# Residual rows placed in PSUM ahead of the first expert, XR as a weight slot, and other orders on VectorE and ScalarE around the groups of heads

## The reference

```python
x = x + g1 * yx                                  # residual of the first block
h2 = modulate(rms_norm(x, norm2_g), sh2, sc2)
x = x + g2 * expert_choice_moe(h2, w_router, w_gate, w_up, w_down)
x = rms_norm(x, final_g)

def expert_choice_moe(h, w_router, w_gate, w_up, w_down):
    aff = softmax(h @ w_router)                  # 256 tokens x 16 experts
    top_w, top_i = top_k(aff.T, 32)              # 32 tokens of each expert
    xg = h[top_i]
    y = (silu(xg @ w_gate) * (xg @ w_up)) @ w_down
    return zeros.at[top_i].add(y * top_w)

def hybrid_mixer(h, ...):                        # each layer of the second block
    z = h @ w_in
    o_mla = mla_attention(q_nope, q_rope, k_nope, k_rope, v_mla)
    o_dil = dilated_attention(rope(qd), rope(kd), vd)
    return concat([rmsnorm(o_mla), rmsnorm(o_dil)]) @ w_out
```

## Time and profile before

| | |
|---|---|
| median of 3 runs | 2342.73 us (2342.62 to 2346.84) |
| the profiled execution's own time | 2353.84 us, span 2352.5 us |
| mean granted clock of TensorE | 0.902 |
| PE busy | 2030.9 us, 86% |
| VectorE busy | 960.3 us, 41% |
| ScalarE busy | 650.2 us, 28% |
| DMA | 647.46 MB, mean 275 GB/s |
| chain that ended last | PE 52%, DMA 34%, VectorE 8% |

### The profile page before, as it was taken

How to read it: one execution, slowest core, us unless ns; L and a number is a source line. 1 busy time by engine, 2 the same in 40 slices (tenths; PEclk the granted TensorE clock), 3 DMA queues, 4 the chain that set the end, 5 groups by cost and what they waited for, 6 DMA issues and landing times.

```text
span 2352.5 us, 29084 instructions
## 1 busy us (share of the span) xinstructions
PE 2030.9 (86%) x12314; PEld 1353.1 (58%) x12314; DVE 960.3 (41%) x1182; ACT 650.2 (28%) x779; POOL 67.4 (3%) x144
## 2 busy tenths in 40 slices
PE   7999999666666666666778999999999999999998
PEld 4767862111111111111136998778998999778997
DVE  3744431000000000000004657866658666876656
ACT  3423210000000000000003444545445444455444
POOL 0000000000000000000001000000001000100000
PEclk9999999787777777777789999989999999999999
DMA  7355789999999999999998564325554554415552
GB/s 301 118 186 193 301 339 405 420 421 420 420 421 421 421 420 420 421 421 421 420 421 323 190 213 155 130 99 180 191 194 153 189 196 161 177 50 199 200 183 95
DMA packets 91361, 647.46 MB, mean 275 GB/s; under 512 B 10144, under 2 KB 10656, under 8 KB 14304
## 3 DMA queue, kind: packets, MB, share of 16 engines
q1 hardware_dynamic: 91232, 645.61, 70.3%
HBM read 644.52 MB, written 1.05 MB: 274 GB/s over the span
## 4 chain that ended last, share of the span: by engine, by line
PE 52%; DMA 34%; DVE 8%; SPq 2%; ACT 1%; issue 1%; POOL 0%; DVEq 0%; ACTq 0%; POOLq 0%
PE PS L429 13%; PE PS L431 13%; PE PS L430 13%; DMA ring<-in_md 6%; DMA ring<-in_mu 6%; DMA ahead<-in_mu 2%; DMA XT<-in_mu 2%; SPq L2752 2%; PE PS L913 2%; DVE low L1798 2%; PE PS L818 1%; PE PS L784 1%; DMA QT<-in_md 1%; DMA HRI<-in_md 1%; DMA XT<-in_md 1%
## 5 line engine op out<-in xcount | busy, mean ns | idle before, releaser
L1798 DVE TENSOR_TENSOR low<-ring,WH 128x2048 fp32r<-128x2048 f32 (+1 forms) x163 | 372.1, 2283 | 181.1 <-ACT WH L2185 178.5
L429 PE MATMUL PS<-XH,WH 128*128 128x256 f32 x1408 | 396.5, 282 | 3.6 <-DVE XL L1829 3.6
L430 PE MATMUL PS<-XL,WH 128*128 128x256 f32 x1408 | 395.0, 281 | 0.0
L431 PE MATMUL PS<-XH,low 128*128 128x256 f32 x1408 | 393.0, 279 | 0.0
L2185 ACT ACTIVATE WH<-ring 128x2048 fp32r<-128x2048 f32 (+1 forms) x164 | 313.3, 1911 | 27.1 <-DMA ring<-in_fg 21.6
L429 PEld LDWEIGHTS PS<-XH,WH 128*128 128x128 f32 x1408 | 264.5, 188 | 7.2 <-issue 5.4
L431 PEld LDWEIGHTS PS<-XH,low 128*128 128x128 f32 x1408 | 267.2, 190 | 0.0
L430 PEld LDWEIGHTS PS<-XL,WH 128*128 128x128 f32 x1408 | 264.3, 188 | 1.4
L1780 DVE TENSOR_TENSOR T1S<-T1S,PS 128x512 f32<-128x512 f32 x16 | 11.0, 688 | 532.1 <-PE PS L878 532.1
L2435 ACT ACTIVATE T1S<-PS 128x512 f32<-128x512 f32 x16 | 9.6, 597 | 548.6 <-PE PS L878 548.6
L429 PE MATMUL PS<-WH,FH 128*128 128x512 f32 x352 | 139.7, 397 | 0.4 <-DVE FL L1927 0.4
(11 more groups left out here) (435 smaller groups left out, 3033.4 us busy)
## 6 DMA issues: line engine op xcount, KB each, us to landing
ring<-in_fg SPq DMA_DIRECT2D x44, 1024.0 KB, 4.9
ring<-in_fu SPq DMA_DIRECT2D x44, 1024.0 KB, 4.9
ring<-in_fd SPq DMA_DIRECT2D x44, 1024.0 KB, 4.8
ring<-in_md SPq DMA_DIRECT2D x43, 1024.0 KB, 27.1
ring<-in_mu SPq DMA_DIRECT2D x39, 1024.0 KB, 27.0
ring<-in_mg SPq DMA_DIRECT2D x38, 1024.0 KB, 27.5
ring<-in_wmod SPq DMA_DIRECT2D x24, 1024.0 KB, 6.5
ahead<-in_mg SPq DMA_DIRECT2D x14, 1024.0 KB, 27.3
```

What stands on the lines that cost most here:

```text
L429: t.matmul(o, l[0], r[0], start=start, stop=False, skip_group_check=True)
L430: t.matmul(o, l[0], r[1], start=False, stop=False, skip_group_check=True)
L431: return t.matmul(o, l[1], r[0], start=False, stop=stop, skip_group_check=True)
L1798: own(v.tensor_tensor(low[:, w.slot.index, 0:size], w.flat, WH[:, w.slot.index, 0:size].bitcast(f32), ALU.subtract).then_inc(*c.wl.up()), ...
```

## The change

The residual rows are added into banks 4 to 7 ahead of the first expert, as the products that open the sums (`start=True`), while VectorE selects the tokens; all experts then add to them. For this the banks 4 to 7 must be free then: the router's logits move to banks 0 and 2, the transposed softmax to bank 1, and the gathered rows to banks 1, 2 and 3, the second half of them evicted by VectorE alone. The fillers around these steps are 3, 12 and 3 where they were 8, 28 and 3. XR is then free during the experts and becomes the twentieth slot of `rest`, behind XT; its semaphore is that of the later row loads, which count on from it.

In the second block VectorE splits the fifth tile of `wid` behind the rotation of q instead of ahead of q's eviction, and the third and fourth tile of `wo2` in the groups 8 and 10 instead of 6 and 8, behind `low_rows`. ScalarE writes the high part of the first half of the rows (`rows(0, 0, 4)`) ahead of the second half of the values instead of behind it. PE transposes the first `dilated_heads` into bank 6 and then bank 7 instead of 7 and 6, so that ScalarE gets the first pair of heads and VectorE the second.

The diff, with its context cut and twelve columns of indentation taken off:

```diff
--- before.py
+++ after.py
@@ -293,7 +293,8 @@
 (ATG[:, 0:2048], c.l_ctx, (c.xr, 4), 1),
-(flat(XT[:, :, :]), c.wide6, (c.rt, 3)))]
+(flat(XT[:, :, :]), c.wide6, (c.rt, 3)),
+(flat(XR[:, :, :]), c.l_row, (c.wo, 9)))]
@@ -352,9 +353,10 @@
 load_expert(slot)
-        rest = wide[4:10] + slots + wide[10:13] + wide[0:4]
+        rest = wide[4:10] + slots + wide[10:14] + wide[0:4]
         for n in range(384 - 8):
 load_expert(rest[n % len(rest)])
+        row_slot[0].loads = wide[13].loads
         last_load = {id(s): n for n, w in enumerate(queue) for s in narrow if s.last is w}
@@ -802,7 +804,7 @@
     for k in range(4 * h, 4 * h + 4):
-        x = t.matmul(PS[:, 4 + m, 0:16], XT[:, k, m * 128:m * 128 + 128], wrA[:, k, :],
+        x = t.matmul(PS[:, 2 * m, 0:16], XT[:, k, m * 128:m * 128 + 128], wrA[:, k, :],
                      start=k == 0, stop=k == 7, skip_group_check=True)
@@ -820,8 +822,6 @@
             if n == 1 and m == 1 and k == 3:
-                take(4)
-                take(5)
                 logits(0, 0)
@@ -833,22 +833,28 @@
 logits(1, 1)
-for b in range(3):
-    held[b] = [(c.xta, 8)]
-held[3] = [(c.xtv, 7)]
-take(7)
-turn_over(6, 8)
+held[0], held[1], held[2], held[3] = [(c.rtv, 1)], [(c.xta, 8)], [(c.rtv, 2)], [(c.xtv, 7)]
+take(1)
+turn_over(6, 3)
 P.wait_ge(c.rtv, 3)
 for m in range(2):
-    x = t.transpose(PS[0:16, 7, m * 128:m * 128 + 128], aff[:, m, :], ident)
+    x = t.transpose(PS[0:16, 1, m * 128:m * 128 + 128], aff[:, m, :], ident)
 x.then_inc(*c.rt.up())
-turn_over(6, 28)
+turn_over(6, 12)
+
+P.wait_ge(c.xna, 4)
+for m in range(2):
+    for n in range(2):
+        take(4 + 2 * m + n)
+        x = t.matmul(PS[:, 4 + 2 * m + n, :], ident[:, :], XR[:, m, n * 512:n * 512 + 512],
+                     start=True, stop=False, skip_group_check=True)
+x.then_inc(*c.wo.up())
 take(3)
...
 x.then_inc(*c.rt.up())
-turn_over(6, 3)
+turn_over(0, 3)
@@ -861,7 +867,7 @@
 for k in range(8):
-    x = gather(k, 0, 2, (6, 5, 2, 4)[k // 4 * 2 + k % 2], (k % 4) // 2 * 64)
+    x = gather(k, 0, 2, 3 if k > 3 else 2 - k % 2, k * 64 - 128 if k > 3 else k // 2 * 64)
     if k % 4 == 3:
@@ -873,7 +879,7 @@
                 P.wait_ge(c.xgv, 1 + k // 4)
-                P.wait_ge(c.xga, 1 + k // 4)
+                P.wait_ge(c.xga, 1)
             for j in range(4):
@@ -883,14 +889,14 @@
                 if k > 1:
-                    P.wait_ge(*((c.xga, 2 + k // 2) if k % 2 else (c.xgv, 2 + k // 2)))
+                    P.wait_ge(*((c.xga, 1 + k // 2) if k % 2 else (c.xgv, 2 + k // 2)))
                 else:
...
         P.wait_ge(c.xgv, 6)
-        P.wait_ge(c.xga, 6)
+        P.wait_ge(c.xga, 5)
     P.wait_ge(c.rp, ex + 1)
@@ -918,18 +924,12 @@
             turn_over(3, 6)
-    if ex == 2:
-        P.wait_ge(c.xr, 4)
-        for m in range(2):
-            for n in range(2):
-                t.matmul(PS[:, 4 + 2 * m + n, :], ident[:, :], XR[:, m, n * 512:n * 512 + 512],
-                         start=False, stop=False, skip_group_check=True)
     P.wait_ge(c.pw, ex + 1)
...
             x = t.matmul(PS[:, 4 + 2 * m + n, :], PB[:, 0, m * 128:m * 128 + 128], T1[:, n * 512:n * 512 + 512],
-                         start=ex == 0, stop=ex == 15, skip_group_check=True)
+                         start=False, stop=ex == 15, skip_group_check=True)
         if n or ex == 15:
@@ -1077,7 +1077,7 @@
             x.then_inc(*c.dq.up())
-            held[at] = [(c.dqa if b else c.dqv, 2 * l + i + 1)]
+            held[at] = [(c.dqa if b == i else c.dqv, 2 * l + i + 1)]
@@ -1150,7 +1150,7 @@
     latent_heads()
-    dilated_heads(0, (7, 6))
+    dilated_heads(0, (6, 7))
@@ -1670,7 +1670,7 @@
     lg = aff[:, m, :]
-    own(v.scalar_tensor_tensor(lg, PS[:, 4 + m, 0:16], stat[:, m:m + 1], cB, ALU.mult, ALU.add))
+    own(v.scalar_tensor_tensor(lg, PS[:, 2 * m, 0:16], stat[:, m:m + 1], cB, ALU.mult, ALU.add))
     own(v.tensor_reduce(r1[:, m:m + 1], lg.rearrange("p (h e) -> p h e", h=1), X, ALU.max,
@@ -1702,7 +1702,7 @@
 R = T2[0:16, :].rearrange("p (a b) -> p a b", a=4)
-av = PS[0:16, 7, 0:256]
+av = PS[0:16, 1, 0:256]
 eq, w_, gt, w2 = (R[:, i, :] for i in range(4))
@@ -1731,10 +1731,16 @@
 own(one_hot(1, 0, 2).then_inc(*c.oh.up()), c.oh)
-for h in range(2):
-    V.wait_ge(c.gx, h + 1)
-    own(second_affine(4 * h, XG0[:, 4 * h, :], PS[:, 6 - 4 * h, 0:64]))
-    own(second_affine(4 * h + 2, XG0[:, 4 * h + 2, :], PS[:, 6 - 4 * h, 64:128]).then_inc(*c.xgv.up()), c.xgv)
+V.wait_ge(c.gx, 1)
+own(second_affine(0, XG0[:, 0, :], PS[:, 2, 0:64]))
+own(second_affine(2, XG0[:, 2, :], PS[:, 2, 64:128]).then_inc(*c.xgv.up()), c.xgv)
+V.wait_ge(c.gx, 2)
+for k in range(4, 8):
+    i = second_affine(k, XG0[:, k, :], PS[:, 3, k * 64 - 128:k * 64 - 64])
+    if k == 7:
+        own(i.then_inc(*c.xgv.up()), c.xgv)
+    else:
+        own(i)
 for m in range(2):
@@ -1994,8 +2000,9 @@
     def dilated_heads(i, b):
-        V.wait_ge(c.dq, 4 * l + 2 * i + 1)
-        own(v.tensor_copy(DT[:, i, 0:2, :].rearrange("p a b -> p (a b)"), PS[:, b, :]).then_inc(*c.dqv.up()), c.dqv)
+        h = 0 if i else 2
+        V.wait_ge(c.dq, 4 * l + 2 * i + h // 2 + 1)
+        own(v.tensor_copy(DT[:, i, h:h + 2, :].rearrange("p a b -> p (a b)"), PS[:, b, :]).then_inc(*c.dqv.up()), c.dqv)
@@ -2034,7 +2041,6 @@
     dilated(1, 0, 6)
-    split_to(tile("wid", 6 * l) + 5)
     q_up(0, 2)
@@ -2045,6 +2051,7 @@
             own(i)
+    split_to(tile("wid", 6 * l) + 5)
     latent_heads()
@@ -2106,10 +2113,10 @@
             normed({4: 1, 8: 5, 10: 7}[g])
-        if g in (2, 4, 6, 8):
-            split_to(tile("wo2", 4 * l) + g // 2)
         if g in (6, 10):
             low_rows(g // 10, 0, 0 if g == 10 else 4)
+        if g in (2, 4, 8, 10):
+            split_to(tile("wo2", 4 * l) + {2: 1, 4: 2, 8: 3, 10: 4}[g])
         if g == 5:
@@ -2420,10 +2427,9 @@
-for h in range(2):
-    A.wait_ge(c.gx, h + 1)
-    own(second_affine(4 * h + 1, XG0[:, 4 * h + 1, :], PS[:, 5 - h, 0:64]))
-    own(second_affine(4 * h + 3, XG0[:, 4 * h + 3, :], PS[:, 5 - h, 64:128]).then_inc(*c.xga.up()), c.xga)
+A.wait_ge(c.gx, 1)
+own(second_affine(1, XG0[:, 1, :], PS[:, 1, 0:64]))
+own(second_affine(3, XG0[:, 3, :], PS[:, 1, 64:128]).then_inc(*c.xga.up()), c.xga)
 for ex in range(16):
@@ -2522,8 +2528,9 @@
     def dilated_heads(i, b):
-        A.wait_ge(c.dq, 4 * l + 2 * i + 2)
-        own(copy(DT[:, i, 2:4, :].rearrange("p a b -> p (a b)"), PS[:, b, :]).then_inc(*c.dqa.up()), c.dqa)
+        h = 2 if i else 0
+        A.wait_ge(c.dq, 4 * l + 2 * i + h // 2 + 1)
+        own(copy(DT[:, i, h:h + 2, :].rearrange("p a b -> p (a b)"), PS[:, b, :]).then_inc(*c.dqa.up()), c.dqa)
@@ -2598,14 +2605,16 @@
             exps(g + 1)
+        if g == 6:
+            rows(0, 0, 4)
         if g in (2, 6):
...
             squared(g // 9, g // 7 % 2 if g < 9 else 0)
-        if g in (6, 10, 11):
-            rows(*{6: (0, 0, 4), 10: (1, 0, 0), 11: (0, 1, 1)}[g])
+        if g in (10, 11):
+            rows(*{10: (1, 0, 0), 11: (0, 1, 1)}[g])
     squared(1, 1)
...
     def ple_rows(i):
```

## The result

| | before | after |
|---|---|---|
| median of 8 runs each, same chip | 2346.05 us (2341.25 to 2351.81) | 2336.27 us (2334.17 to 2338.53) |
| profiled execution | 2353.84 us, span 2352.5 | 2335.08 us, span 2333.8 |
| mean granted clock | 0.902 | 0.908 |

The ratio is 0.9958, interval 0.9945 to 0.9971: faster, by 0.4%. The prediction was 2334.5 us, range 2330 to 2341. Between the two profiled executions the span fell by 18.7 us, as the sum had it; between the medians the time fell by 9.8 us, where I had 8.3.

The account below looks back on a forecast made before the run. It took the weight stream to bound the experts, and PE with its waits the second block. Terms: 18.7 us off the profiled execution gives 2335.1, 8.3 off the 2342.73 median gives 2334.4; forecast 2334.5 us, range 2330 to 2341.

Parts of the forecast that it names:

- 18.7: Whole kernel: predicted gain in us against the profiled execution, 3.3 + 2 x 0.8 + 2 x 1.7 + 10.4.
- The stream: First expert: XR as twentieth slot and an earlier restart close the weight stream's gap, gaining 3.3 us.
- my head start of 1.2: Router: with fewer fillers the softmax transposes, selection and first expert come 1.2 us earlier.
- The split behind q: Second block, both layers: moving VectorE's split behind q's rotation removes PE's 0.82 us wait, gaining 0.8 us a layer.
- The bank swap: Second block, first dilated_heads: swapping banks 6 and 7 gains 0, at most 0.3 us.
- The XL order: Head group with XL: the new order removes 1.9 of PE's 2.00 us wait; less 0.2 new waits, 1.7 a layer.
- The clock: Behind the XL wait, both layers: without the wait no falls to half clock are expected, gaining 10.4 us.
- the two theories: Experiments' question: each part gives its wait's cost (the sum), or clock dominates and nearly all comes from the XL order.
- no fall behind the waits of 0.2 to 1.0 us: Rival, second block: the clock falls anyway, there or behind another PE wait of about 1 us; 2343.3 us, chance 0.13.
- PE not late to the first expert: Rival, first expert: PE comes late by what the tile bought, the stream gains nothing; 2337.8 us, chance 0.08.
- VectorE not the bound: Rival, head groups: VectorE becomes the bound and the 1.7 us a layer don't come; 2337.9 us, chance 0.08.
- no wait at the last copy: Rival, last copy of turned weights: the split delays it, PE waits up to 2 us, clock falls; 2356 us, chance 0.05.

Follow-up runs that it names:

- heads_only: The kernel before with only the second block's part of the change: 2337.62 us, ratio 0.9963 to the kernel before.
- no_slot: The changed kernel with XR left out of the slots, 19 instead of twenty: 2337.53 us, ratio 0.9965 to the kernel before.
- old_fillers: The changed kernel with 8 and 28 fillers where it has 3 and 12: 2337.88 us, ratio 0.996 to the kernel before.
- moe_only: The kernel before with only the first block's part of the change: 2343.4 us against 2345.6, ratio 0.9995.
- xl_undone: The changed kernel with only the order around XL put back on VectorE and ScalarE: 2344.79 us, ratio 0.9985 to the kernel before.
- after_again: The changed kernel run once more, unchanged, in the second group: 2335.6 us, ratio 0.9952 to the kernel before.
- no_fillers: The changed kernel without its 3, 12 and 3 fillers at the router: 2336.39 us, ratio 0.9958 to the kernel before.
- banks_undone: The changed kernel with only banks 6 and 7 and the head pairs of the first dilated_heads put back: 2334.97 us, ratio 0.9945 to the kernel before.
- q_undone: The changed kernel with only VectorE's split of the fifth wid tile back ahead of q's eviction: 2337.24 us, ratio 0.9954 to the kernel before.

## Why the prediction was right

**The stream: right against the profiled execution, a third too large against one at full clock.** Counted from XT's issue to the first gate tile's landing, the stretch took 926.5 us before, 925.1 without the first-block part (heads_only), 925.2 with it but no slot (no_slot), and 923.2 with slot (after). The other kernels with the slot and with short fillers or none had 922.3 to 923.9, old_fillers 926.0. Against the profiled execution of before the gain is 3.2 us, where I had 3.3. It has two parts. The slot, with what goes with it, takes 1.2 to 2.9 us off 925.1 or 925.2, about 2.0 in the middle; I had 2.5 for it without a head start. The shorter fillers take the rest, 926.5 - 925.2 = 1.3 between before and no_slot, both at low clock: my head start of 1.2. But that part is there only where the clock is low at the router, as it was in the profiled execution of before; heads_only, with all fillers and at full clock, restarts as early as the kernel after. I read 16 slow fillers as the rule, and they are the rule of about two executions in three, by the 13 profiles. So against a run of before at full clock the term that I took whole into the median, 3.3, was mis-sized: about 2.0 is what the traces show. The times do not show the stream's gain by itself: moe_only is not told apart from before. That the residual products cost PE nothing is right at this filler count alone, as old_fillers shows.

**The split behind q: right.** The stretch from VectorE's first work behind PE's q products (the split before, q's evictions after) to the first turned heads was 1503.09 - 1492.04 = 11.05 us and is 1498.33 - 1488.01 = 10.32: 0.73 a layer, against 0.8; undone, it costs 1.6 us across groups and 2.3 within one, for both layers. The bank swap: 0 predicted, and nothing that the medians tell apart (0.6 us).

**The XL order: right.** 2.00 - 0.21 = 1.8 us a layer against 1.7. The cover at the last copy of turned weights is used up, as said, with no new wait on PE there.

**The clock: right in the profiled execution, and misread for the median.** The stretches behind XL are 8.8 and 1.6 us shorter, the two figures for the falls. xl_undone shows the cause as far as it is the order: with the old order back, both waits and both falls come back. But I took the median of before to be runs without falls. Over its 12 to 35 runs in a group its median was 2345.6 to 2347.9, 3 to 5 us above the first three runs' 2342.73, while its fastest were 2341.3 to 2341.7. So the usual run of it seems to hold part of the low clock, and the gain of 9.8 us is larger than the 8.3 that I summed for the waits and the gap. Between the fastest runs it is 2341.25 - 2334.17 = 7.1 us, near what is left when the stream term is set to 2.0: 2.0 + 1.5 + 3.6 = 7.1. So close an agreement is chance, though: by the fastest runs of the first group heads_only gains 6.6 us, where the waits are 5.1, and moe_only loses 0.5. The spread says the same as the medians: 10.6 us before, 8.4 with the XL order undone, 4.4 after.

**How exact 18.7 is.** That the span fell by just the sum is in part luck. 0.9 us of it came ahead of the change's reach (XT's issue), 3.2 from the stream, and 14.6 from the second block, where the terms had 15.4.

**What the medians and the profiles add up to.** By medians heads_only gained 8.0 us and moe_only 2.2, together 10.2, near 9.8. But undoing the two orders one by one costs 9.2 + 1.6 = 10.8, more than heads_only gained, and xl_undone, which keeps the q order and the slot, is only 1.1 us under before. The profiled executions do add up. From the first gate tile's landing to the end of the span it is 1073.6 to 1075.5 us in the seven with the q and XL orders of the change (heads_only, no_slot, old_fillers, after, after_again, no_fillers, banks_undone). Before took 1089.6, at least 14.1 more; xl_undone 1084.7, at least 9.2; moe_only 1082.5, at least 7.0. In before 23.5 us at half clock cost 10.4, so 0.44 us for each. With the waits (3.6 for XL, 1.5 for q) and an estimate at that price for the 13.6 us at half in xl_undone and the 3.4 in moe_only, the three come to 15.5, 9.6 and 6.6, the last 0.4 short of what was measured. q_undone took 1077.8, at least 2.3 more, where its waits are 1.6. So in the profiled executions the waits and the time at half clock account for nearly all. Of the two theories it is the sum that holds, once the clock is one of its terms, and the largest: 10.4 of before's 15.5. That the medians differ by how much low clock their runs hold follows from that, but is not shown: only one run of each kernel was profiled.

**Rivals.** Of the four, none came: no fall behind the waits of 0.2 to 1.0 us that stayed in the heads; PE not late to the first expert at full clock, though moe_only kept a third of the gap in a profiled run whose clock was at half from 336 to 343; VectorE not the bound; no wait at the last copy. By the Trainium skill ("TensorE: Matmul & The Clock Gate", HAM oscillation) the 2.0 us wait should have been harmless. Here a fall followed it in 5 of 6 profiled occurrences (twice before, twice in xl_undone, once in moe_only), and in the ten profiles with the new XL order no 5 us window of the second block shows a lower clock until PE's last products, though waits up to 1.5 us stayed. The measurement decides. A fall needs no such wait, however, as the router shows (last section).

## What to carry to other kernels

Before pricing a wait on PE, look at the clock in the windows behind it: here a wait of 2.0 us cost 1.8 us by itself and as much again or more in the clock, and it was removed by moving 2.3 us splits on VectorE and one small copy on ScalarE. Before pricing something by a stretch of the trace, look at the clock in it too: a head start read at low clock was not there at full clock. And one profile is one execution: here a second one of the same code had another clock at the router. A prefetch slot is worth only what the work put in its way leaves: measure slot and work together, since here neither alone showed in the time.

## What the runs showed of the hardware

- The low clock behind a 2.0 us wait did not last a fixed time: 20.3 us in layer 0 and 3.2 in layer 1 of before, 3.4 us (2 x 5 x 0.34) and 10.2 in xl_undone, none at all behind one of two such waits in moe_only and 3.4 behind the other.
- The clock also fell where PE had hardly waited. In the router of before, PE's only wait from 318 to 337 us was 0.34 us; it had run the 16 logit products (128x16) and was in the fillers when the clock fell. heads_only ran the same code with the same wait and kept 1.00. The row of the fall in before:

```profile
336.00:337.00 1.00, 1.00 (x9) 0.90 1.05 434
```

- In no_fillers the clock was at half from about 337.3 to 344.1, with PE nearly idle from 335 to 339.5 and the residual products running behind that, and back at 1.00 while they still ran. The time shows 0.8 us of it, since the work lay beside VectorE's.
- Between issue and first data behind an idle queue: heads_only issues at 351.08, moves nothing from 351 to 352.0, about 0.12 MB from 352.0 to 352.25, next to nothing from there to 353, and runs at full rate from 353 on. So the first data came 0.9 to 1.2 us after the issue and the full rate 1.9 us after it. Before issues at 353.53, has its first data between 354.25 and 354.5 (0.7 to 1.0 us) and the full rate from about 355.5. The 1.7 us that the prediction set against a first byte is thus nearer to the time to the full rate, which is what a restart needs.
